# A fused two-layer trunk in one kernel: the norm totals made for all partitions at once, root and reciprocal on whole tiles

## The reference, cut to what matters

```python
def rmsnorm(x, w):
    y = x * lax.rsqrt(jnp.mean(x * x, axis=-1, keepdims=True) + EPS)
    return y * w

u = modulate(rmsnorm(h, norm_w), shift, scale)       # x * (1 + scale) + shift
h = h + 0.5 * gate * ((silu(u @ wg) * (u @ wu)) @ wd)   # ffn_half
...
h = h + gate * mixer(u, ...)
```

## Time and profile before

| | |
|---|---|
| median of 3 runs | 1967.5 us (1966.04 to 1969.38) |
| profiled execution | 1963.97 us, span 1962.3 us |
| TensorE matmul busy | 1940.1 us, 99% of the span |
| VectorE busy | 1258.4 us, 64% |
| ScalarE busy | 790.1 us, 40% |
| mean granted TensorE clock | 0.998 of full speed |
| HBM traffic | 146 GB/s over the span |

### The profile page before, as it was taken

One profiled execution on the slowest core, in us unless ns is written; L12 is line 12 of the kernel. 1 busy time (PEld: TensorE's weight loads), 2 busy tenths in 40 slices (PEclk: granted clock), 3 DMA queues, 4 the chain that ended last, 5 costly groups with the idle time before them and its releaser, 6 DMA issues.

```text
span 1962.3 us, 28467 instructions
## 1 busy us (share of the span) xinstructions
PE 1940.1 (99%) x9802; PEld 1640.8 (84%) x9802; DVE 1258.4 (64%) x2037; ACT 790.1 (40%) x1089; POOL 73.4 (4%) x144
## 2 busy tenths in 40 slices
PE   9999999999999999999999999999999999999998
PEld 5788888888888888888888888888888888899997
DVE  5666576667665466667566666765857678576555
ACT  4322322346554323532222354223134567455444
POOL 0000000000000000000000000000100000000000
PEclk9999999999999999999999999999999999999999
DMA  7445454433123243345444424544543333455554
GB/s 282 157 152 182 139 182 161 151 117 106 67 65 113 96 140 118 108 141 202 139 161 162 166 98 139 182 161 140 185 154 133 103 102 106 168 172 183 186 189 150
DMA packets 78680, 287.39 MB, mean 146 GB/s; under 512 B 8904, under 2 KB 9168, under 8 KB 77968
## 3 DMA queue, kind: packets, MB, share of 16 engines
q1 hardware_dynamic: 58464, 212.37, 32.3%
q0 software_dynamic: 19568, 73.35, 11.3%
q10 hardware_dynamic: 576, 0.70, 0.1%
HBM read 285.34 MB, written 1.05 MB: 146 GB/s over the span
## 4 chain that ended last, share of the span: by engine, by line
PE 93%; DVE 2%; DMA 2%; ACT 1%; issue 1%; ACTq 0%; SPq 0%; DVEq 0%; POOL 0%; POOLq 0%
PE bank L385 26%; PE bank L386 26%; PE bank L387 26%; DMA raw<-weights 2%; PE bank L634 2%; PE bank L694 1%; PE bank L688 1%; PE bank L689 1%; PE bank L552 1%; PE bank L554 1%; PE bank L555 1%; PE bank L405 1%; ACT w_hi L846 1%; PE bank L771 1%; PE bank L430 1%
## 5 line engine op out<-in xcount | busy, mean ns | idle before, releaser
L385 PE MATMUL bank<-u_hi,w_hi 128*128 128x512 f32 (+1 forms) x1824 | 664.8, 364 | 0.3 <-DVE w_lo L1172 0.3
L387 PE MATMUL bank<-u_hi,w_lo 128*128 128x512 f32 (+1 forms) x1824 | 655.7, 359 | 0.0
L386 PE MATMUL bank<-u_lo,w_hi 128*128 128x512 f32 (+1 forms) x1824 | 655.6, 359 | 0.0
L1172 DVE TENSOR_TENSOR w_lo<-raw,w_hi 128x1024 fp32r<-128x1024 f32 x382 | 466.6, 1223 | 250.8 <-ACT w_hi L846 222.5
L846 ACT ACTIVATE w_hi<-raw 128x1024 fp32r<-128x1024 f32 x382 | 402.8, 1055 | 440.3 <-DMA raw<-weights 436.5
L385 PEld LDWEIGHTS bank<-u_hi,w_hi 128*128 128x128 f32 x1824 | 345.0, 189 | 50.8 <-issue 0.7
L387 PEld LDWEIGHTS bank<-u_hi,w_lo 128*128 128x128 f32 x1824 | 344.7, 189 | 51.1
L386 PEld LDWEIGHTS bank<-u_lo,w_hi 128*128 128x128 f32 x1824 | 345.0, 189 | 50.0 <-issue 0.7
L1183 DVE SCALAR_TENSOR_TENSOR junk<-ada_raw,silu_c 128x1024 bf16<-128x1024 f32 x256 | 298.1, 1221 | 0.0
L385 PE MATMUL bank<-hid_hi,w_hi 128*128 128x512 f32 (+1 forms) x656 | 249.4, 380 | 0.0
L387 PE MATMUL bank<-hid_hi,w_lo 128*128 128x512 f32 (+1 forms) x656 | 248.8, 379 | 0.0
(11 more groups left out here) (194 smaller groups left out, 1670.6 us busy)
## 6 DMA issues: line engine op xcount, KB each, us to landing
raw<-weights SPq DMA_DIRECT2D x382, 512.0 KB, 3.5
ada_raw<-adaw POOLq DMA_DIRECT2D x128, 512.0 KB, 4.3
start_g<-weights SPq DMA_DIRECT2D x14, 512.0 KB, 12.7
box<-box POOLq DMA_DIRECT2D x4, 1024.0 KB, 7.9
h<-resid SPq DMA_DIRECT2D x4, 512.0 KB, 8.3
silu_c<-c SPq DMA_DIRECT2D x1, 1024.0 KB, 16.8
start_r<-weights SPq DMA_DIRECT2D x2, 512.0 KB, 17.0
poolw<-poolw POOLq DMA_DIRECT2D x2, 256.0 KB, 9.7
```

What stands on the lines that cost most here:

```text
L385: pe.matmul(ps, w_hi[:, slot, k, :], hi(k), start=first, stop=False)
L386: pe.matmul(ps, w_hi[:, slot, k, :], lo(k), start=False, stop=False)
L387: mm = pe.matmul(ps, w_lo[:, slot, k, :], hi(k), start=False, stop=last)
L1172: dve.tensor_tensor(view(w_lo, (j % RING) * UNIT, [1, UNIT]), raw[:, j % RING, :], view(w_hi, (j % RING) * UNIT, [1, UNIT]).bitcast(F32), ...
```

## The change

A full square of ones is now the stationary operand of the totals, and the squares are the moving one, so each stream's total arrives on all partitions and for all 256 tokens at once. The root and the reciprocal are taken on those 128x256 tiles (`rstd`, in the place of `diag`). The diagonal, the spreading matmul and its counter are gone, and `norm_t` reads `rstd` instead of a bank. The fillers are (2, 8) instead of (2, 3, 5). In norm 0 start columns 0, start group 1's last piece and start group 2's first piece follow the totals directly, the last of them behind a wait for both roots. The fourth row bank is 5 instead of 4.

```diff
-KEEP_BUSY = (2, 3, 5)
-ROW_BANK = (6, 7, 3, 4)
+KEEP_BUSY = (2, 8)
+ROW_BANK = (6, 7, 3, 5)
...
-        diag, _ = sb("diag", [P, ALL // P, P], F32, scan_at[1] + 6144)
+        rstd, _ = sb("rstd", [P, ALL], F32, scan_at[1] + 6144)
...
                 for s in range(nstream):
-                    for t in range(2):
-                        pe.matmul(bank[4 + 2 * s][:, t:t + 1], sq_sum[:, s * TOK + t * P:s * TOK + (t + 1) * P],
-                                  ones[:, 0:1], start=(t == 0), stop=False, skip_group_check=True)
+                    pe.matmul(bank[4 + 2 * s][:, 0:TOK], ones[:], sq_sum[:, span(s)], start=True, stop=False,
+                              skip_group_check=True)
                 keep_busy(n, KEEP_BUSY[0])
                 residual_rows(n, 0, 5)
                 for s in range(nstream):
                     pe.wait_ge(s_sq, sq_count(n) + ND + s)
-                    for t in range(2):
-                        mm = pe.matmul(bank[4 + 2 * s][:, t:t + 1], sq[:, 1, s * TOK + t * P:s * TOK + (t + 1) * P],
-                                       ones[:, 0:1], start=False, stop=True, skip_group_check=True)
-                    mm.then_inc(s_ssq, 1)
+                    pe.matmul(bank[4 + 2 * s][:, 0:TOK], ones[:], sq[:, 1, span(s)], start=False, stop=True,
+                              skip_group_check=True).then_inc(s_ssq, 1)
                 if n == 0:
                     start_group(1, range(2, 3))
-                keep_busy(n, KEEP_BUSY[1])
-                residual_rows(n, 5, 9)
-                for s in range(nstream):
-                    pe.wait_ge(s_diag, stream_count(n) + s + 1)
-                    pe.matmul(bank[5 + 2 * s][:, 0:TOK], ones[:], view(diag, s * TOK, [1, TOK]), start=True, stop=True
-                              ).then_inc(s_bc, 1)
-                if n == 0:
                     start_columns(0)
                     start_group(1, range(3, 4))
+                    pe.wait_ge(s_std, 2)
                     start_group(2, range(1))
-                keep_busy(n, KEEP_BUSY[2])
-                residual_rows(n, 9, 16)
+                keep_busy(n, KEEP_BUSY[1])
+                residual_rows(n, 5, 16)
...
-                    act.activation(r_cols[:, 0, 2 * s:2 * s + 2], bank[4 + 2 * s][:, 0:2], ACT.Sqrt, bias=eps_c[:],
+                    act.activation(rstd[:, span(s)], bank[4 + 2 * s][:, 0:TOK], ACT.Sqrt, bias=eps_c[:],
                                    scale=1.0 / D).then_inc(s_std, 1)
...
-                    spread(r_cols[:, 0, 2 * s:2 * s + 2], diag, s * TOK, TOK).then_inc(s_diag, 1)
+                    dve.reciprocal(rstd[:, span(s)], rstd[:, span(s)]).then_inc(s_rstd, 1)
...
-                                                       scalar=scale_c[:, s, d:d + 1], in1=bank[5 + 2 * s][:, 0:TOK],
+                                                       scalar=scale_c[:, s, d:d + 1], in1=rstd[:, span(s)],
```

More of the change, by code:

```diff
@@ L230, in program @@
         s_std = sem("std_ready")
-        s_diag = sem("diag_ready")
-        s_bc = sem("rstd_spread")
+        s_rstd = sem("rstd_ready")
         s_nt = sem("normed")
@@ L1259, in scaled @@
                         if d == 0:
-                            dve.wait_ge(s_bc, stream_count(n) + s + 1)
+                            dve.wait_ge(s_rstd, stream_count(n) + s + 1)
                         dve.scalar_tensor_tensor(out=norm_t[:, d % 4, span(s)], in0=h[:, d, span(s)],
-                                                       scalar=scale_c[:, s, d:d + 1], in1=bank[5 + 2 * s][:, 0:TOK],
+                                                       scalar=scale_c[:, s, d:d + 1], in1=rstd[:, span(s)],
                                                        op0=ALU.mult, op1=ALU.mult).then_inc(s_nt, 2 * TOK // nt)
```

## The result

The changed kernel took 1980.38 us in the median of 5 runs (1977.74 to 1985.26), against 1967.5 before: ratio 1.0078, 95% interval 1.0064 to 1.0091. The ratio is not the quotient of these two medians, which is 1.0065: it would put the kernel before at 1965.1, and in the three later sets of runs that kernel did take 1965.2 to 1965.7. So the change costs 12.9 us by the first medians and some 15 by the ratio. Two executions of the kernel before fell out of line, at 5046.57 us, for which the record has no cause, and at 2025.18 with a mean clock of 0.917 in a later set; no reading here rests on them. The prediction was 1983.8 in a range of 1974.3 to 1991.

A forecast was written before the change was run, and what follows sets the result against it. TensorE's matmuls were taken to bound the kernel, with each norm an exposed chain. Chain +11.8 and clock +4.5 gave +16.3, taking the profiled 1963.97 to 1980.3; the median lay 3.5 higher, so 1983.8 us, range 1974.3 to 1991.

The forecast's parts named there:

- That nothing later takes the delay back: After each norm: weight loads, splits and modulation dot products wait on counters that move along with TensorE.
- Totals +0.08: Totals matmuls in each norm: equal time on the chain, but the last one's consumer starts 0.08 us later.
- root +0.12: ScalarE's root on 128x256 out of a bank: root and hand-over grow from 0.30 to 0.42 us.
- Reading `rstd` from SBUF: `norm_t` in each norm, reading `rstd` in SBUF instead of the bank: no change in time.
- R = 1.99: VectorE's whole-tile reciprocal in each norm: 1.99 us at 7.2 ns a column, twice in order where there are two streams.
- The upper bound of 2.26: VectorE's whole-tile reciprocal: at most 2.26 us, from 203 ns and 8.3 ns for each of 248 more columns.
- The chain's sum, +11.8: Six norms together: 2.6 each in norms 1, 2, 4, 1.0 in norm 3, 2.3 in norm 0, 0.7 in norm 5.
- The clock, +4.5: TensorE's clock falling in the gaps of norms 0 to 4: three falls in four, 1.2 us each.
- The prediction's bound of 1.7 for one fall: TensorE behind a norm's gap: one fall costs at most 1.7 us, 3.4 us of real work at half speed.
- A half-clock stretch beyond 3.4 us: TensorE's granted clock in the profile: a half-clock stretch lasting beyond the 3.4 us seen would make the forecast wrong.
- That the reciprocal runs at an ordinary element's rate: Rival on VectorE's whole-tile reciprocal: R = 0.42 us, -5.4 us over the norms, 1962.1 us; chance 0.05.
- That the clock holds (1979.3): Rival on TensorE's gaps in the norms: no clock falls, only the chain's +11.8, 1979.3 us; chance 0.23.

The follow-up runs named there:

- e6_widths: The kernel before with one extra reciprocal per stream behind the diagonals, 256 columns wide in norm 0, 16, 32, 64, 128, 8 in norms 1 to 5: 6.26 ns a column.
- e1_constant: The changed kernel with each of the eleven whole-tile reciprocals replaced by a one-pass operation (times 0, plus 0.004): 1961.1 us, ratio 0.9977.
- the versions with fillers: The changed kernel with 19 fillers instead of 8 behind the totals and 13 in norm 0, run twice: 1978.54 and 1977.8 us, ratios 1.0059 and 1.0062.
- e2_fillers: The changed kernel with 19 fillers instead of 8 behind the totals and 13 in norm 0, first run: 1978.54 us, ratio 1.0059.
- both one-root profiles: The changed kernel with root and reciprocal in one ScalarE operation and 5 fillers instead of 8, run twice: 1957.42 and 1956.97 us, ratios 0.9956 and 0.996.
- without fillers: The changed kernel without the eight fillers behind the totals, the two ahead of them kept: 1979.77 us, ratio 1.0075.

## Why the prediction was right, step by step

**The forecast as a whole: right, 3.4 us too high.** It was built on the median of 1967.5 shown then; the later sets put the kernel before some 2 us lower, so that a rise of 16.3 was forecast and one of 12.9 (medians) to 15 (ratio) came.

**That nothing later takes the delay back: right.** The stages behind norms 1 and 2 lengthened by exactly the distance to work once the clock held (1.83 and 1.93 for 1.84 and 1.88).

**Totals +0.08 and root +0.12: right in size.** First totals to root went from 1.94 to 1.99 us in norm 1 and from 1.90 to 1.99 in norms 2 and 4, root to reciprocal from 0.30 to 0.50 (0.42 expected: the root takes 473 ns, not the 381 of a copy). Together 0.25 to 0.3 for 0.20. **Reading `rstd` from SBUF: nothing**, as expected (473 ns against 476).

**The reciprocal, R = 1.99: right in kind, 0.3 us too high.** It took 1.73 in the mean, and two in a row 3.37, so 1.68 each in the sum. The slope of 7.2 ns came from 2 and 8 columns, where the short operations lie off the line; the true one is 6.26 (e6_widths). The upper bound of 2.26 was above the measured 1.73. So was the estimate of 2.3 us, by 8 cycles an element, from the Trainium skill (VectorE: DVE Perf Modes, "First, the fixed hardware budget"); that page's iterated divide fits the trace in kind, since a one-pass operation on the same tile took 0.29 us (e1_constant). Eleven times 0.3 is 3.4 us of the sum.

**The chain's sum, +11.8: measured +8.1.** By the distances to work: norm 0 +1.7 (2.3 expected), norms 1, 2 and 4 +1.8, 1.9 and 1.9 (2.6), norm 3 +0.05 (1.0), norm 5 +0.7 (0.7). The difference of 3.7 is the reciprocal's size, all but 0.3.

**The clock, +4.5: right in kind, near in size, with one bound broken.** A fall was expected to cost 1.2 us three times in four in five norms. Measured: 1.5 to 1.6 us behind norms 1 and 2, 3.5 in norm 0 in the one profile where it fell there, at four of the five norms in the first profile of the changed kernel and three in each of the others. That is some 8 us in the first and 4.6 in the others. The prediction's bound of 1.7 for one fall was too low for norm 0: the clock stayed at half for 10.2 us there, not 3.4. A half-clock stretch beyond 3.4 us was one of the signs by which the prediction called itself wrong; it came, in one profile in three, and the range still held because the reciprocal was cheaper than forecast. In the kernel's time the fillers give 3.2 us back. The falls also go with the spread of the changed kernel's runs, 7.5 us: within its first five, 1977.7 and 1978.0 us came with a mean clock of 0.996, 1983.5 and 1985.3 with 0.994 and 0.993.

**What is left over.** Of the 15 us by the ratio 8.1 are chain and 3.2 what fillers give back; 4 are left, and in the versions with fillers, 12.6 and 13.2 us above the kernel before of their sets, 4.5 to 5. (By the first medians it would be 1.6 for the changed kernel, but its base lies 2 us above the later ones.) The profiles put it into the mixer of layer 1, from norm 4's first real matmul to norm 5's totals. That stretch in the kernel before, the changed one (1st and 2nd) and e2_fillers:

```profile
1516.92:1761.63 244.71, 233.80 (x1555) 214.28 (x1553) 176.43 (x387) 145.22 (x236) 1.58 (x3) 1.00 0.39 128
1533.88:1782.13 248.25, 235.54 (x1552) 215.39 (x1552) 176.80 (x387) 145.81 (x236) 1.58 (x3) 0.99 0.39 127
1529.80:1773.85 244.05, 233.57 (x1552) 214.18 (x1552) 176.68 (x387) 145.50 (x236) 1.58 (x3) 1.00 0.41 129
1525.19:1774.47 249.28, 235.68 (x1553) 215.50 (x1553) 176.47 (x387) 145.11 (x236) 1.58 (x3) 0.99 0.39 126
```

The excess has two parts. In the profiles with a 3.4 us fall in the stretch TensorE is busy 1.2 to 2.2 us longer (235.2 to 235.8 us, against 233.6 to 234.0 without one). The rest is idle time: 10.9 us before, 12.7, 10.5 and 12.0 in the three profiles of the changed kernel, 13.6 and 13.2 with the fillers. The largest wait, for `pv`, is 2.81 us in the first profile and 1.62 before, and ahead of it ScalarE waits 3.62 us for a weight unit to land, before 2.45. The clock fell inside the mixer in the first profile of the changed kernel, in both with fillers and in e1_constant (stretch 247.3 us), behind waits of 1.8 to 2.8 us; before, in the second profile of the changed kernel and in both one-root profiles (244.0) it did not. So the leftover is waits on late weights and a fall behind them, and neither needs the reciprocals, since e1_constant has both. Whether any part of the change makes the weights land later, or it is chance in so few profiles, stays open.

**The rivals.** That the reciprocal runs at an ordinary element's rate would have given 1962.1; e1_constant, where an ordinary operation takes its place, measured 1961.1. The agreement within 1 us is in part luck: the distances to work shrink by 5.1 us there (forecast 5.4, with 0.8 in norm 0 that did not come and 2.5 instead of 2.1 in norm 3), while the base was 2 us too high and the mixer took 2.6 us longer. The rival's condition does not hold. That the clock holds (1979.3) came within 1 us of e2_fillers, by errors that cancel: a chain 3.7 us too long and a base 2 us too high against the mixer's 4.6 us and 0.4 in norm 4.

## What to carry to other kernels

Moving a computation from a column to a whole tile is free only for operations whose price is nearly all fixed. Ask the trace for the same operation at two widths, and take the slope from wide ones: here 2 and 8 columns gave 7.2 ns a column and 16 to 256 gave 6.3. If the operation is slow per element, keep it on the column, or put it into an operation that passes over the tile anyway. And count a gap on TensorE at its length plus what half clock may cost behind it, which comes in some executions and not in others. Here the one operation for root and reciprocal, where its precision is enough, turned a loss of 0.8% into a gain of 0.4%.

## What the runs showed of the hardware

- VectorE's reciprocal in f32 costs 6.26 ns a column from 16 columns up, with 118 ns of fixed cost: 218, 318, 519, 919 and 1721 ns at 16, 32, 64, 128 and 256. A one-pass operation on the same SBUF tile took 294.
- TensorE's clock fell to half in or behind gaps of 2.7 us, 4.5 us, and 1.3 and 0.9 us in succession, and in the mixer behind waits of 1.8 to 2.8 us. It did not fall behind the same 2.7 us gap in other norms and profiles. In norm 1 of the changed kernel it was at full speed during the gap (414 to 416) and fell 0.5 us into the work; in norm 0 of that profile and in norms 3 and 4 without fillers it fell 0.7 to 1.7 us before the work began. Behind norms 1 and 2 a fall lasted 3.4 us and cost 1.5 to 1.6; the one of 6.8 us in norm 3 cost 2.3, the one of 10.2 us in norm 0 cost 3.5. The Trainium skill (TensorE: Matmul & The Clock Gate, "What's actually happening") knows the two speeds, and the traces show no third.
- Root and reciprocal in one ScalarE operation on 128x256 took 473 ns, as much as the root alone.
